# Even and odd mixers: output projections ended two tiles at a time, values and head chains ahead, narrow products wide, gelu in one piece

## What is computed

```python
def even_mixer(h, ...):
    z = h @ w_in                                   # 1024 -> 1696
    u, v = gelu(z[..., :512]), gelu(z[..., 512:1024])
    a = spatial_gating(u, v, ...)                  # rmsnorm(v) by 4 groups, mixed over
                                                   # 128 tokens by w_s, + b_s, times u
    b = mla(z[..., 1024:1408], z[..., 1408:1664], z[..., 1664:], ...)
    return concatenate([a, b], -1) @ w_out         # 1024 -> 1024

def mla(c_q, c_kv, k_pe, ...):
    q = (rmsnorm(c_q) @ w_uq)                      # 8 heads of 96
    kv = (rmsnorm(c_kv) @ w_ukv)                   # 8 heads of 64 + 64
    k = concatenate([kv[..., :64], k_pe of every head])
    q, k = rmsnorm(q), rmsnorm(k); rope on their last 32
    return block_causal_attention(q, k, kv[..., 64:])

def odd_mixer(h, ...):
    z = h @ w_in                                   # 1024 -> 6144
    q, k = rope(z[..., :1024]), rope(z[..., 1024:2048])       # 4 heads of 256
    v, g = z[..., 2048:4096], z[..., 4096:]                   # 4 heads of 512
    o = rmsnorm(retention(q, k, v), out_norm)
    return (o * silu(g)) @ w_out                   # 2048 -> 1024

x = x + mixer(rmsnorm(x)); h = rmsnorm(x)
x = x + (silu(h @ w_gate) * (h @ w_up)) @ w_down
```

## Time and profile before

| | |
|---|---|
| median of 3 runs | 2555.53 us (2553.45 to 2555.55) |
| the profiled execution: its own time | 2554.28 us |
| its span | 2552.2 us |
| mean granted clock of TensorE | 0.974 of 2.4 GHz |
| busy: PE, PEld, DVE, ACT, POOL | 95%, 87%, 71%, 51%, 5% |
| chain that ended last | PE 86%, DVE 9%, ACT 4% |

### The profile page before, as it was taken

One profiled execution on the slowest core, in us unless ns is written; L12 is line 12 of the kernel. 1 busy time (PEld: TensorE's weight loads), 2 busy tenths in 40 slices (PEclk: granted clock), 3 DMA queues, 4 the chain that ended last, 5 costly groups with the idle time before them and its releaser, 6 DMA issues.

```text
span 2552.2 us, 39046 instructions
## 1 busy us (share of the span) xinstructions
PE 2431.1 (95%) x15856; PEld 2221.0 (87%) x15856; DVE 1801.2 (71%) x2679; ACT 1304.5 (51%) x1995; POOL 115.7 (5%) x104
## 2 busy tenths in 40 slices
PE   7789999989999999889998999999998899989998
PEld 7678889887888888889998888898888899988887
DVE  4659757567867876777467876688767664678864
ACT  5545454545544544556454554455445663545543
POOL 0002100001200000210000000000002100000000
PEclk9899999999999999999999999999999899999999
DMA  5236565344656565533253656556664332446652
GB/s 182 83 112 213 180 209 181 129 133 144 191 185 198 190 187 185 179 122 108 92 164 126 206 185 187 166 187 198 186 187 160 112 111 97 158 134 204 188 175 91
DMA packets 114882, 409.92 MB, mean 161 GB/s; under 512 B 12816, under 2 KB 14992, under 8 KB 114704
## 3 DMA queue, kind: packets, MB, share of 16 engines
q1 hardware_dynamic: 114704, 407.43, 49.9%
HBM read 406.33 MB, written 1.05 MB: 160 GB/s over the span
## 4 chain that ended last, share of the span: by engine, by line
PE 86%; DVE 9%; ACT 4%; issue 1%; DMA 0%; SPq 0%; ACTq 0%; DVEq 0%
PE ps L359 85%; DVE wlo L1655 3%; ACT whi L1007 1%; ACT region L1170 1%; PE ps L568 0%; DVE x L1812 0%; DVE x L1830 0%; DVE region L1855 0%; DVE xx L1710 0%; DVE region L1950 0%; DMA cst<-in_consts 0%; DVE region L2226 0%; DVE region L2184 0%; DVE region L2312 0%; DVE region L2223 0%
## 5 line engine op out<-in xcount | busy, mean ns | idle before, releaser
L359 PE MATMUL ps<-xx,whi 128*128 128x256 f32 (+1 forms) x4912 | 1346.9, 345 | 40.5 <-ACT region L1404 16.1
L1655 DVE TENSOR_TENSOR wlo<-raw,whi 128x1024 fp32r<-128x1024 f32 (+3 forms) x772 | 935.6, 1217 | 444.5 <-ACT whi L1007 442.9
L1007 ACT ACTIVATE whi<-raw 128x1024 fp32r<-128x1024 f32 (+3 forms) x772 | 800.7, 1043 | 531.4 <-PE ps L359 531.0
L359 PE MATMUL ps<-xx,wlo 128*128 128x256 f32 x3688 | 1046.3, 284 | 0.0
L359 PEld LDWEIGHTS ps<-xx,whi 128*128 128x128 f32 x4912 | 864.8, 193 | 156.5 <-ACT region L1404 16.5
L359 PEld LDWEIGHTS ps<-xx,wlo 128*128 128x128 f32 x3688 | 709.9, 192 | 0.3
L359 PE MATMUL ps<-H,whi 128*128 128x512 f32 (+1 forms) x2400 | 686.7, 351 | 22.1 <-DVE wlo L1655 10.4
L359 PE MATMUL ps<-H,wlo 128*128 128x256 f32 x1888 | 534.7, 283 | 0.0
L359 PEld LDWEIGHTS ps<-H,whi 128*128 128x128 f32 x2400 | 425.5, 191 | 86.4 <-issue 14.6
L359 PEld LDWEIGHTS ps<-H,wlo 128*128 128x128 f32 x1888 | 358.9, 190 | 0.2
L1650 DVE TENSOR_REDUCE t<-ps 128x256 f32<-128x512 f32 x308 | 211.7, 689 | 51.5 <-PE ps L359 42.4
(11 more groups left out here) (271 smaller groups left out, 1564.0 us busy)
## 6 DMA issues: line engine op xcount, KB each, us to landing
raw<-in_sg SPq DMA_DIRECT2D x128, 512.0 KB, 3.8
raw<-in_su SPq DMA_DIRECT2D x128, 512.0 KB, 3.5
raw<-in_sd SPq DMA_DIRECT2D x128, 512.0 KB, 3.9
raw<-in_mw_g SPq DMA_DIRECT2D x48, 512.0 KB, 3.5
raw<-in_fg SPq DMA_DIRECT2D x44, 512.0 KB, 3.4
raw<-in_fu SPq DMA_DIRECT2D x44, 512.0 KB, 3.6
raw<-in_fd SPq DMA_DIRECT2D x32, 512.0 KB, 3.5
raw<-in_mw_a SPq DMA_DIRECT2D x24, 512.0 KB, 3.8
```

Source lines behind the costliest of these rows:

```text
L359: return e.matmul(out, lhsT, rhs, start=start, stop=stop, skip_group_check=True)
L1007: e.activation(m.whi[:, c % NHL, 0:cw], m.raw[:, c % NRAW, 0:cw], ACT.Copy).then_inc(s["whi"].h, s["whi"].up(c))
L1655: e.tensor_tensor(m.wlo[:, c % NHL, 0:cw], m.raw[:, c % NRAW, 0:cw], m.whi[:, c % NHL, 0:cw].bitcast(F32), ALU.subtract).then_inc(s["wlo"] ...
```

## The change

In the order of the program:

1. x is lowered after two weight chunks instead of four, and ScalarE loads its first table before the first weight has landed. The first step computes two latent tiles, the others one at a time.
2. `k_pe` is computed feature by token: 8 matmuls of 512 columns and 8 of 256, with a sum on VectorE and two transposes back. Squares are added on VectorE first, so that 4 one-column products are left of 10.
3. Two of the four value chunks move ahead of k, v and q, into banks 6 and 7. All later steps of the head chains stand one or two tiles closer.
4. Gelu of u is one instruction over four tiles behind the last of them. The gated tiles are lowered one behind.
5. In `ew_out` two steps fall on each of the first four chunks. The last four chunks hold the same weights in another layout (`out` in `lay_out`): each has two output tiles with all four remaining blocks. So `gemm_last` ends a pair of tiles with each chunk. `ow_out` likewise with its last four of 16.
6. The feed-forwards of these two layers start in banks 4 to 7 (`first_bank`), with the statistics in bank 3 and one more chunk converted before them.
7. Heads of the odd mixer start at gate chunks 0, 7 and 14 and at output chunk 4, with more bare steps between their pieces.

```diff
 def weight_order():
-    o = [("ew_c", i) for i in range(5)] + [("ew_pe", 0)]
+    o = [("ew_c", i) for i in range(5)] + [("ew_pe", 0), ("ew_v", 0), ("ew_v", 1)]
     for half in range(2):
         o += [("ew_ukv", half)] + [("ew_uq", 3 * half + i) for i in range(3)]
-    o += [("ew_v", i) for i in range(4)] + [("ew_u", i) for i in range(4)] + [("ew_out", i) for i in range(8)]
+    o += [("ew_v", 2), ("ew_v", 3)] + [("ew_u", i) for i in range(4)] + [("ew_out", i) for i in range(8)]
...
+def first_bank(kind, j):
+    return 2 * ((j + (2 if kind == "rms" else 0)) % 4)
...
+    def gemm_last(name, i, tag, hb):
+        for p in range(4):
+            wh, wl = weights(name, i + p)
+            for n in range(2):
+                o = ps[p][:, n * 256:n * 256 + 256]
+                for k in range(4):
+                    w.wait_ge(s["hlo"], *tag(k))
+                    c = (n * 4 + k) * 128
+                    t = mm3(o, wh[:, c:c + 128], wl[:, c:c + 128], hb[0][:, k, :], hb[1][:, k, :], False, k == 3)
+            t.then_inc(s["gemm"].h, s["gemm"].up(name, i + p))
...
     def even():
-        gemm_first("e", [("ew_c", i, take(i, ("edve", "lat", i))[:, 0:256]) for i in range(4)])
+        gemm_first("e", [("ew_c", i, take(i, ("edve", "lat", i))[:, 0:256]) for i in range(2)])
+        gemm_fm("ew_c", 2, take(2, ("edve", "lat", 2))[:, 0:256], xh, xl)
         rms_stats("e", RT=True)
-        gemm_fm("ew_c", 4, take(4, ("edve", "lat", 4))[:, 0:256], xh, xl)
-        gemm_tm("ew_pe", 0, [take(5, ("edve", "kpe"))], xh, xl, 8, 8, 32)
+        for i in range(3, 5):
+            gemm_fm("ew_c", i, take(i, ("edve", "lat", i))[:, 0:256], xh, xl)
+        wh, wl = weights("ew_pe", 0)
+        b = take(5, ("edve", "kpf"))
+        for k in range(8):
+            c = slice(k * 32, k * 32 + 32)
+            mm(b[0:32, :], wh[:, c], m.xx[:, k].rearrange("p a b -> p (a b)"), start=k == 0, stop=False)
+            t = mm(b[0:32, 0:256], wl[:, c], xh[:, k, :], start=False, stop=True)
...
+        value(0)
+        w.wait_ge(s["edve"], "kpf")
...
+        value(1)
...
-        gemm_tm("ew_v", 0, [take(2 + tt, ("eact", "v", tt)) for tt in range(2)], xh, xl, 8, 2, 512, after=side.step)
+        for c in (2, 3):
+            value(c)
+            side.step()
...
         for k in range(4):
             w.wait_ge(s["hlo"], "ea", k)
-            gemm_acc("ew_out", k, h1[0], h1[1], k, k == 0, False, readers)
-            side.step()
-        for k in range(4):
-            side.until(lambda: k in ot)
-            w.wait_ge(s["hlo"], "eo", k)
-            gemm_acc("ew_out", 4 + k, h2[0], h2[1], k, False, k == 3, readers)
+            gemm_acc("ew_out", k, h1[0], h1[1], k, k == 0, readers, side.step)
             side.step()
         side.finish()
+        gemm_last("ew_out", 4, lambda k: ("eo", k), h2)
...
     def odd():
...
         for i in range(16):
             gemm_fm("ow_g", i, take(i % 4, ("rdve", "g", i))[:, 0:256], xh, xl)
-            if i in (6, 12):
-                side.add(head(0 if i == 6 else 1))
+            if i in (0, 7, 14):
+                side.add(head(i // 7))
+            side.step()
+        readers = [[("xadd", "f1", p)] for p in range(4)]
+        for c in range(12):
+            h, k = c // 4, c % 4
+            w.wait_ge(s["hlo"], "o", c)
+            gemm_acc("ow_out", c, hb[h % 2][0], hb[h % 2][1], k, c == 0, readers)
+            if c == 4:
+                side.add(head(3))
             side.step()
         side.finish()
...
+        gemm_last("ow_out", 12, lambda k: ("o", 12 + k), h2)
...
     def rms_parts(st, gname, xin):
...
+        if st == "e":
+            produce(2)
         prefetch(ACT.Sqrt)
...
         if kind == "rms":
-            rms_stats(st, nxt=ACT.Silu)
+            produce(1)
+            rms_stats(st, nxt=ACT.Silu, bank=3)
...
         for i in range(4):
             chunk()
-            w.wait_ge(s["edve"], "u", i)
-            e.activation(m.euF[:, i, :], m.euF[:, i, :], ACT.Gelu_apprx_tanh).then_inc(s["eact"].h, s["eact"].up("u", i))
...
+            if i == 3:
+                w.wait_ge(s["edve"], "u", 3)
+                e.activation(m.euF[:, :, :], m.euF[:, :, :], ACT.Gelu_apprx_tanh).then_inc(s["eact"].h, s["eact"].up("u"))
             side.step()
...
     def add_pair(st, p, alpha, gemm):
         v = x[:, 2 * p:2 * p + 2, :]
-        w.wait_ge(s["gemm"], *(gemm if p == 3 else ("pair", gemm[0], p)))
+        w.wait_ge(s["gemm"], gemm[0], gemm[1] + p)
...
+    def out(w):
+        last = w[-512:].reshape(4, 128, 4, 2, 128).transpose(2, 1, 3, 0, 4).reshape(4, 128, 1024)
+        return np.concatenate([w[:-512].reshape(-1, 128, 1024), last])
```

More of the change, by code:

```diff
@@ L428, in gemm_tm, with gemm_acc @@
                 after()
-    def gemm_acc(name, i, ah, al, k, first, last, readers):
+    def gemm_acc(name, i, ah, al, k, first, readers, half=None):
         wh, wl = weights(name, i)
@@ L686, in odd @@
         hb = [h1, h2]
-        ot = set()
         def head(h):
@@ L1303, in even @@
             side.step()
-        for k in range(4):
-            side.until(lambda: k in ot)
-            chunk()
             side.step()
         side.finish()
+        for _ in range(4):
+            chunk()
     def odd():
@@ L1356, in odd @@
             e.activation(m.sg[:, i, :], m.sg[:, i, :], ACT.Silu).then_inc(s["ract"].h, s["ract"].up("g", i))
-            if i in (6, 12):
-                side.add(head(0 if i == 6 else 1))
+            if i in (0, 7, 14):
+                side.add(head(i // 7))
+            side.step()
+        for c in range(12):
+            chunk()
+            if c == 4:
+                side.add(head(3))
             side.step()
         side.finish()
-        for h in range(4):
-            if h < 3 and h + 1 not in ot:
-                side.add(head(h + 1))
-            for k in range(4):
-                if k == 0 and h not in ot:
-                    side.finish()
-                chunk()
-                side.step()
-            side.finish()
+        for _ in range(4):
+            chunk()
     def hybrid(l):
@@ L2093, in even @@
         side.add(heads(1))
-        for _ in range(4):
+        for _ in range(2):
             chunk()
@@ L2182, in head, with gated @@
                 s["rdve"].h, s["rdve"].up("sq", h))
-            w.wait_ge(s["ract"], "root", h)
-            e.reciprocal(m.Ro[:, 1, :], m.Ro[:, 0, :]).then_inc(s["rdve"].h, s["rdve"].up("r", h))
             yield
-            w.wait_ge(s["rdve"], "r", h)
-            for q in range(4):
+            yield
+            def gated(q):
                 i = h * 4 + q
@@ L2194, in head @@
                     s["rdve"].h, s["rdve"].up("y", h, q))
[L2195 to L2196 removed]
+            w.wait_ge(s["ract"], "root", h)
+            e.reciprocal(m.Ro[:, 1, :], m.Ro[:, 0, :]).then_inc(s["rdve"].h, s["rdve"].up("r", h))
+            w.wait_ge(s["rdve"], "r", h)
+            for q in range(2):
+                gated(q)
+            yield
+            for q in range(2, 4):
+                gated(q)
+            for q in range(4):
+                if q == 2:
                     yield
[L2198 removed]
+                low(hb[h % 2][1][:, q, :], m.o[:, q, :], hb[h % 2][0][:, q, :], ("hhi", "hlo"), "o", h * 4 + q)
         for i in range(16):
```

178 lines of the change are left out of this document (101 added, 77 removed).

## The result

The changed kernel takes 2522.15 us (median of 4 runs, 2520.33 to 2523.24), the one before 2555.54: a ratio of 0.9866, 95% interval 0.9848 to 0.9884. The forecast was 2523. Its profiled execution has a span of 2518.5 us against 2552.2.

The account below looks back on a forecast made before the run. TensorE, busy 95% of the span, was taken as the bound, so its waits and low-clock work count. Gains of 14.8 + 17.8 = 32.6 us took the profiled 2554.28 to 2521.7, 2523 against the median; range 2508 to 2540.

Parts of the forecast that it names:

- the first half of the change: Even mixer and first feed-forward entry: start 10.5 us earlier, plus 2.8 and 1.5 in the entry, 14.8 us.
- The term behind it: Narrow products at the even mixer's start: wide k_pe and fewer one-column products save 6.9 us, plus 1.5 of slow clock.
- The waits of 5.2 (L2102) and 3.6 (one of L1673) have gone and left 1.2: Even mixer, before the first output tile: it starts at 103.5 instead of 121.02, with 1.2 us of waits left.
- rival (a): Only the ends count, waits inside the mixers just change place: 19 us gained in all, 2536.5; 24%.
- gelu in one piece: Even mixer: without table loads of 1.28 us among exponentials, gelu ends at 98.8 and the first output tile follows at 103.5.
- end 3 us apart: Feed-forward entries: tile pairs ending apart, with banks 4 to 7, leave a wait of 1.0 us instead of 6.7.
- Both waits for wlo go: Feed-forward entries: one more tile lowered ahead of the statistics removes both waits for wlo, 3.1 us together.
- waits at the first output tile: Odd mixer: TensorE reaches the first output tile at 501.5 and waits 1.3 and 3.2 us for the last gates.
- Behind that nothing binds: Odd mixer, after the first output tile: the last two heads have 3 us or more of slack.
- (b): Chains overlap better than in the walk: half the remaining mixer waits gone gives 2507, all 2491; 12%.
- (c): Banks don't free the entries, since something else ends as late as the fourth addition: 11.4 us stay, 2534; 8%.
- (d): Slower: the lower clock follows the merged 10 us wait in the even mixer, 53 us more, 2576; 3%.

Follow-up runs that it names:

- e4: Changed kernel with k_pe as 48 products of 32 columns again, without the sum on VectorE and the two transposes back; 2530.14 us.
- e9: Changed kernel with old last chunks and the even mixer behind k_pe in the old order (values, gelu, gated tiles, head steps); 2523.5 us.
- e6: Changed kernel with gelu of u as four instructions of 256 columns, one behind each u tile, instead of one of 1024; 2525.29 us.
- e2: Changed kernel with the last four weight chunks of both output projections in the old layout, new banks kept; 2520.0 us.
- e7: Changed kernel with the odd mixer's heads and steps scheduled as before the change, ending and banks as changed; 2536.74 us.
- e10: Changed kernel with the old last chunks and the old schedule of the odd mixer's heads; 2530.41 us.
- e8: Changed kernel unchanged, profiled a second time; 2522.66 us.
- e12: e11 with the evacuation of the third and fourth heads' scores moved ahead of a weight, a u tile and the normalised values on VectorE; 2511.95 us.
- e11: Changed kernel with old last chunks, second value chunk behind q, and VectorE's q and k squares and scaling ahead of weights; 2516.26 us.
- e1: Changed kernel with the feed-forwards of both layers starting in banks 0 to 3 again, statistics in bank 7; 2538.05 us.
- e3: Changed kernel with both the old layout of the last chunks and the old banks; 2534.23 us.
- e5: Changed kernel with the second of the two early value chunks moved back behind the q products of both halves; 2518.57 us.

## Why the prediction came out right, and where it did not

The time, 2523 against 2522.15, is closer than its steps. In the touched pieces the profiles show 35.7 and 33.4 us of gain where 32.6 were summed; the hybrid layers, which are "left alone by the change", gave back 2.8 and 1.1, of which 2.4 in the first profile are the clock of the one place shown above. Errors of both signs met, and that the sum came within 1 us is luck: the first half of the change was forecast at 14.8 and gave 18.2, the second at 17.8 and gave 17.5.

**Start of the even mixer.** Right in every time: first product at 14.06 (forecast 14), rotation waited for until 72.65 (72.9) with 10.2 in one piece. The term behind it is right in size with the wrong split. The 48 products of 32 columns took 6.6 of the 10.9 us, of which 5.3 are their price at the full clock (0.11 each, e4); the rest of the 10.9 went on one-column products, all at the lower clock:

```profile
41.48 4.41 PE L359 MATMUL ps<-cst,region 128*128 128x1 f32 x20
```

```profile
41.14 0.95 PE L365 MATMUL ps<-cst,region 128*128 128x1 f32 x8
```

The second row is the changed kernel's, with fewer of them and at the full clock. By these steps some 3.4 of the 6.9 us were clock (1.3 in the 48, 2.1 in the others), more than the 1.5 that the forecast gives it.

**Middle of the even mixer.** The second transposes began at 89.9 (90.7), the first output tile at 102.6 (103.5), the waits for transposed scores were 3.9 and 3.0 (4.5 and 5.1), the first ended by VectorE and the second by ScalarE. The mixer ended at 142.5, not 147.4, the largest single miss: 0.9 of it was there at the first output tile, 2.7 came from the last two waits, the rest from the work and the clock behind them, which no run tells apart. "The waits of 5.2 (L2102) and 3.6 (one of L1673) have gone and left 1.2" is true of that place and no gain: rival (a) described this mixer correctly, its idle time is 33.2 us as before, and the order is worth 2 us (e9). The step that gave gelu in one piece a part in it failed outright (e6); ScalarE was idle there.

**Entries.** The forecast had F0 10.5 us earlier with a wait of 1.0 left; measured were a wait of 1.50 (1.35 at the second) and F0 14.9 us earlier, and both entries 3.3 and 2.3 us shorter by the clock and the statistics (forecast 4.3 and 3.3). Of the two causes named only the banks count; that pairs "end 3 us apart" brings nothing (e2). "Both waits for wlo go" failed: they come later, 1.27 and 1.02 us, as VectorE is some weights behind after the additions.

**Odd mixer.** The waits at the first output tile are there, ended by the last gates' scaling, 0.6 and 2.6 us (1.3 and 3.2). "Behind that nothing binds" is not quite so: 1.9 us of waits for lowered output stand there. The gain to the second feed-forward was 15.2 (213.4), in the second profile 13.6, where 14.5 was forecast with its low clock. Early heads carry it (e7, e10).

**Rivals.** (a) holds for the even mixer's middle and nowhere else, and its 2536.5 failed since the odd mixer's waits did go. (b) was partly true in the last stretch of the even mixer. (c) and (d) fell: banks free the entries, and behind the wait of 10.2 us the lower clock lasted only into the transposes.

## What to carry to other kernels

When TensorE waits in the middle of a chain that another engine sets, moving its own work about only changes where it waits; look at what stands in that engine's program between two links of the chain (here weights lowered too early), since taking it out moved everything behind by its full length. Ask of each edit who would take up what it finishes earlier: a pair of tiles was ready 8 us ahead of a reader that stood behind something else, while other bank numbers gave 5 us at each entry at once. And price small products by rows at one clock level.

## What the runs showed of the hardware

**Low clock after narrow products.** TensorE was not idle between 16.34 and 59 us in the kernel before, and its granted clock still fell from 2.4 to 1.2 GHz within the products of 32 columns (at 38.7 us, in e4 at 36.2). So a fall does not need a wait here. That the narrow products are its cause rests on two kernels that have them and twelve profiles without; no other stream was tried.

**Two paces at one clock.** In the second feed-forward, with TensorE busy all the time and the granted clock at 1.00, the same products run at two paces. The window from 800 to 860 us, of the changed kernel and of e2:

```profile
800.00:860.00 60.00, 60.00 (x349) 52.91 (x347) 48.90 (x66) 30.32 (x44) 0.00 (x0) 1.00 0.60 191
```

```profile
800.00:860.00 60.00, 60.00 (x341) 52.04 (x340) 48.11 (x64) 30.27 (x44) 0.00 (x0) 1.00 0.59 188
```

400 products take 70.7 or 69.3 us. The kernel before, the changed one, e7, e8 and e12 go over from the slower pace to the faster between 700 and 780 us and back some 180 us later; e4 has the faster at its start as well, e9 to e11 go from the faster to the slower, and e1, e2, e3, e5 and e6 keep the slower one. The main changes fall on the same products in every profile that has them (near the 1050th and the 2100th of this feed-forward), though at other times. From its 155th product to the end of the hybrid layers' first long wait this makes 464.5 (e4) to 470.8 us of the same instructions. No run was made to find its cause, which stays open. The 6 us between its ends are more than most steps of the experiments, so a difference of two profiles has to be read stage by stage. Whether it also makes one kernel's runs differ is not shown: both profiles of the changed kernel have the same paces.
